# A two-block transformer kernel on one core: the mixer's value weights as ordinary tiles, and the last gate tiles and branch columns in another order

## The reference, cut to what matters

```
z = xn @ w_in[l]                       # 1024 -> 5952 columns
r, k, v, xw, xa, xg = ...              # shifted columns for the RWKV mixer
mq, mk, mv, mo, mi, mf = ...           # columns for the mLSTM mixer
y_a = _rwkv7_mixer(r, k, v, ...)       # a triangular system, solved in levels, then 4 chunks
y_b = _mlstm_mixer(mq, mk, mv, ...)    # 4 heads; mv are the values, needed as (token, column)
g_a, g_b = jnp.split(z_gate, 2, axis=-1)
u = jax.nn.sigmoid(g_a) * (y_a @ br_a[l]) + jax.nn.sigmoid(g_b) * (y_b @ br_b[l])
h = h + u @ w_out[l]
```

## Time and profile before

| what | us |
|---|---|
| time before, median of 3 runs | 2619.52 (2617.49 to 2622.0) |
| the profiled execution's own time | 2617.78 |
| its span in the trace | 2615.8 |
| mixer of layer 0, from tile 27's wait to L2133 | 1439.2 to 1471.5 of the span |
| the same in layer 1 | 2185.7 to 2216.4 |

### The profile page before, as it was taken

The page is one execution under the profiler, slowest core; times in us unless marked ns, Lnnn a source line. Parts: engine busy times, 40 slices in busy tenths (PEclk is TensorE's granted clock), DMA queues, the critical chain, the costliest instruction groups (busy, mean ns, idle before and its releaser), DMA issues.

```text
span 2615.8 us, 50326 instructions
## 1 busy us (share of the span) xinstructions
PE 2434.9 (93%) x20748; PEld 2207.6 (84%) x20748; DVE 1248.7 (48%) x1990; ACT 1002.4 (38%) x1594; POOL 224.7 (9%) x199
## 2 busy tenths in 40 slices
PE   7999799899989799999999799999999987989998
PEld 3754599799966599989998688899999977888998
DVE  1152355555424255465567353455555565443554
ACT  3153433354334353343345331334433454321433
POOL 0000000000000000010005231100100033321000
PEclk9999899989989999989999799999999998999999
DMA  6154354354424545345533112544445231114552
GB/s 256 70 176 174 144 190 172 128 183 178 160 81 166 189 169 191 146 164 186 184 112 108 55 67 106 212 181 180 164 174 191 105 129 65 66 67 161 201 184 96
DMA packets 64486, 388.05 MB, mean 148 GB/s; under 512 B 7152, under 2 KB 7280, under 8 KB 27376
## 3 DMA queue, kind: packets, MB, share of 16 engines
q1 hardware_dynamic: 63216, 379.61, 39.8%
q10 hardware_dynamic: 864, 5.16, 0.5%
q0 software_dynamic: 288, 1.57, 0.2%
HBM read 385.27 MB, written 1.05 MB: 148 GB/s over the span
## 4 chain that ended last, share of the span: by engine, by line
PE 79%; DVE 5%; issue 5%; POOL 4%; ACT 4%; DMA 2%; POOLq 0%; SPq 0%; DVEq 0%; ACTq 0%
PE ps L1707 19%; PE ps L1708 19%; PE ps L1709 19%; PE ps L1783 5%; POOL t_lo L555 3%; PE ps L1796 2%; PE ps L2221 2%; PE ps L2068 2%; DMA ring_a<-in_wa 2%; POOL h_lo L533 1%; PE ps L2259 1%; PE ps L1677 1%; PE ps L2194 1%; PE ps L1654 1%; PE ps L1811 1%
## 5 line engine op out<-in xcount | busy, mean ns | idle before, releaser
L1707 PE MATMUL ps<-h_hi,w_hi 128*128 128x256 f32 x2464 | 702.6, 285 | 12.4 <-DVE mod L1063 8.7
L1708 PE MATMUL ps<-h_lo,w_hi 128*128 128x256 f32 x2464 | 700.5, 284 | 0.0
L1709 PE MATMUL ps<-h_hi,w_lo 128*128 128x256 f32 x2464 | 700.5, 284 | 0.0
L1707 PEld LDWEIGHTS ps<-h_hi,w_hi 128*128 128x128 f32 x2464 | 476.6, 193 | 14.7 <-DVE mod L1063 9.6
L1708 PEld LDWEIGHTS ps<-h_lo,w_hi 128*128 128x128 f32 x2464 | 476.5, 193 | 0.1
L1709 PEld LDWEIGHTS ps<-h_hi,w_lo 128*128 128x128 f32 x2464 | 476.3, 193 | 0.0
L1125 DVE TENSOR_TENSOR w_lo<-ring_a,w_hi 128x1024 fp32r<-128x1024 f32 x308 | 366.4, 1231 | 30.0 <-ACT w_hi L634 29.8
L1708 PE MATMUL ps<-hid_lo,d_hi 128*128 128x256 f32 x1232 | 348.7, 283 | 0.0
L1707 PE MATMUL ps<-hid_hi,d_hi 128*128 128x256 f32 x1232 | 348.7, 283 | 0.0
L1709 PE MATMUL ps<-hid_hi,d_lo 128*128 128x256 f32 x1232 | 348.6, 283 | 0.0
L634 ACT CAST w_hi<-ring_a 128x1024 fp32r<-128x1024 f32 x308 | 306.0, 1044 | 61.9 <-DMA ring_a<-in_wa 61.9
(11 more groups left out here) (282 smaller groups left out, 3296.9 us busy)
## 6 DMA issues: line engine op xcount, KB each, us to landing
ring_a<-in_wa SPq DMA_DIRECT2D x278, 1024.0 KB, 4.8
ring_d<-in_wd SPq DMA_DIRECT2D x154, 512.0 KB, 5.3
work<-in_wa SPq DMA_DIRECT2D x6, 1024.0 KB, 21.7
work<-in_small POOLq DMA_DIRECT2D x2, 768.0 KB, 5.6
c<-in_c ACTq DMA_DIRECT2D x1, 1175.0 KB, 10.4
work<-in_c ACTq DMA_DIRECT2D x1, 1088.0 KB, 5.0
x<-in_x ACTq DMA_DIRECT2D x1, 1024.0 KB, 14.8
work<-in_ctx ACTq DMA_DIRECT2D x1, 1024.0 KB, 19.3
```

The lines of the kernel that those rows point to most:

```text
L1707: nc.tensor.matmul(out, hi, to_hi, start=start, stop=False, skip_group_check=True)
L1708: nc.tensor.matmul(out, hi, to_lo, start=False, stop=False, skip_group_check=True)
L1709: return nc.tensor.matmul(out, lo, to_hi, start=False, stop=stop, skip_group_check=True)
```

## The change

The value tiles 27 to 30 become ordinary tiles: TensorE's `tile` with the weights stationary, ScalarE's `empty_value` into the buffers `sg` and `hid` (`vraw`), then eight transposes into banks 6 and 7, and two copies by ScalarE into `mv` (`mvt`, `mv`). In layer 1 the places of the tiles are moved two ahead as well: tile 23 stands ahead of the head norms (`head_norms`), tiles 24 and 25 between the first transposes and the first `per_unit`. At the end of the mixer both last gate tiles stand ahead of y's transposes, and ScalarE empties both ahead of its root (`ysd`). The branch columns 0 to 3 of `y_b` follow the transposes in four banks. TensorE's wait for `hsd` ahead of the levels is gone.

```diff
-        ems = [v[:, i, :] for v in (sg, hid) for i in range(2)]
+        ems = vraw = [v[:, i, :] for v in (sg, hid) for i in range(2)]
...
-                def empty_values(t):
...
+                def empty_value(t):
+
+                    act.wait_ge(t_done, l * NT2 + t + 1)
+                    nc.scalar.copy(vraw[t - MV], ps[:, 4 + t % 2, 0:T]).then_inc(t_free, 1)
                     round_t(t + 2)
...
-                empty_t(23)
+                def empties(first, last):
+                    for t in range(first, last + 1):
+                        (empty_t if t < MV else empty_value)(t)
+
+                later = 2 * l
+                empties(23, 23 + later)
...
-                empty_values(MV)
+                empties(27 + later, 28)
...
-                empty_values(MV + 2)
+                empties(29, 29)
                 act.wait_ge(ml_v, MVS.at("c3", l))
                 nc.scalar.activation(nsq[:, :, :], nsq[:, :, :], ACT.Silu).then_inc(ml_a, 1)
+                empties(30, 30)
+                act.wait_ge(ml_p, MP.at("mvt", l))
+                for b in range(2):
+                    ins = nc.scalar.copy(mv[:, b, :], ps[:, 6 + b, :])
+                ins.then_inc(ml_a, 1)
...
                 empty_gate(gates_at("y", 0)[0])
+                empty_gate(gates_at("y", 1)[0])
                 act.wait_ge(rw_v, RV.at("s2", l))
...
-                empty_gate(gates_at("y", 1)[0])
...
-                    nc.vector.tensor_tensor(umix[:, n, :], ps[:, 4 + n % 2, 0:T], gate_a[:, n, :], ALU.mult)\
+                    nc.vector.tensor_tensor(umix[:, n, :], ps[:, 4 + n % 4, 0:T], gate_a[:, n, :], ALU.mult)\
...
+                if l:
+                    tile(23)
+                    head_norms()
                 pe.wait_ge(rw_a, RA.at("gg", l))
+                pe.wait_ge(rw_v, RV.at("rkr", l))
                 to_tokens(z[:, V0:V0 + QT, 1:T + 1], 6).then_inc(rw_p, 1)
-                tile(23)
+                if l == 0:
+                    tile(23)
+                else:
+                    tile(24)
+                    tile(25)
...
-                value_tiles(MV)
+                for t in range(n + 3, MV + 2):
+                    tile(t)
...
-                value_tiles(MV + 2)
-
+                tile(29)
+                tile(30)
+                pe.wait_ge(t_free, p0 + GATES)
+                pe.wait_ge(rw_v, RV.at("mt", l))
+                for b in range(2):
+                    for j in range(QT):
+                        mm = nc.tensor.transpose(ps[:, 6 + b, j * P:(j + 1) * P], vraw[j][:, b * P:(b + 1) * P], ident)
+                mm.then_inc(ml_p, 1)
...
-                pe.wait_ge(ml_a, MA.at("hsd", l))
...
                 tile(gates_at("y", 0)[0], bank=6)
-
-                pe.wait_ge(ml_v, MVS.at(f"yb{QT - 1}", l))
-                chunk_here(chunk0[f"br{l}"], chunk0[f"br{l}"] % 2)
-                pe.wait_ge(ch_v, CV.at("s", l * NC_ + NC_ - 1))
-                branch(0, 1)
-                branch(1, 1)
+                tile(gates_at("y", 1)[0], bank=6)
...
-                tile(gates_at("y", 1)[0], bank=6)
+                pe.wait_ge(ml_v, MVS.at(f"yb{QT - 1}", l))
+                pe.wait_ge(ch_v, CV.at("s", l * NC_ + NC_ - 1))
+                for n in range(4):
+                    if n == 2:
+                        pe.wait_ge(t_free, p0 + NT2)
+                    if n % 2 == 0:
+                        chunk_here(chunk0[f"br{l}"] + n // 2, (chunk0[f"br{l}"] + n // 2) % 2)
+                    branch(n, 1)
...
-                    if n >= 2:
+                    if n >= 4:
                         if n % 2 == 0:
                             chunk_here(c, c % 2)
-                        pe.wait_ge(br_free, l * KD + n - 1)
+                        pe.wait_ge(br_free, l * KD + n - 3)
                         branch(n, 1)
```

More of the change, by code:

```diff
@@ L349, in program @@
                     + [f"{n}{j}" for j in range(QT) for n in ("rec", "hs", "yb")])
-        MA = Steps(["ab", "ex", "ln", "silu", "hq", "hsd", "so"])
-        MP = Steps(["if", "mu", "var"])
+        MA = Steps(["ab", "ex", "ln", "silu", "mv", "hq", "hsd", "so"])
+        MP = Steps(["if", "mvt", "mu", "var"])
         n_id = {}
@@ L884, in empty_conv @@
                     round_t(t + 2)
-                def empty_values(t):
-                    act.wait_ge(t_done, l * NT2 + t + 2)
-                    both = ps[:, 5 if t == MV else 4, :].rearrange("p (b s n) -> p s b n", b=2, s=2)
-                    for u in range(2):
-                        j = t + u - MV
-                        nc.scalar.copy(mv[:, :, j * P:(j + 1) * P], both[:, (t + u) % 2]).then_inc(t_free, 1)
+                def empty_value(t):
+                    act.wait_ge(t_done, l * NT2 + t + 1)
+                    nc.scalar.copy(vraw[t - MV], ps[:, 4 + t % 2, 0:T]).then_inc(t_free, 1)
                     round_t(t + 2)
-                    round_t(t + 3)
                 def empty_gate(t):
@@ L1975, in tile @@
                     mm.then_inc(t_done, 1)
-                def value_tiles(t):
-                    pe.wait_ge(t_free, p0 + MV if t > MV else p0 + MV - 1)
-                    for u in range(2):
-                        for part in range(2):
-                            tile_here(t + u, part)
-                    for b in range(2):
-                        for k in range(KD):
-                            cols = slice(b * P, (b + 1) * P)
-                            out = ps[:, 5 if t == MV else 4, b * T:(b + 1) * T].rearrange("p (a n) -> p a n", n=P)
-                            for i, (act_, w) in enumerate(((h_hi, t_hi), (h_lo, t_hi), (h_hi, t_lo))):
-                                mm = nc.tensor.matmul(out, act_[:, k, cols], w[:, :, k, :],
-                                                      start=(k == 0 and i == 0), stop=(k == KD - 1 and i == 2))
-                    mm.then_inc(t_done, 2)
                 for t in range(4):
@@ L2034, in _, with head_norms @@
                     tile(t)
-                pe.wait_ge(rw_v, RV.at("rn", l))
-                if l:
-                    pe.wait_ge(vres_a, 1)
-                hr = const("headrow")
-                for j in range(QT):
-                    mm = nc.tensor.matmul(ps[:, j // 2, half(j)], hr[0:8, cols(j)], inv_norm, start=True, stop=True)
-                mm.then_inc(rw_p, 1)
-                pe.wait_ge(rw_v, RV.at("rkr", l))
-                for j in range(QT):
-                    mm = nc.tensor.matmul(ps[:, 2 + j // 2, half(j)], const("headones"), bon[:, j, :],
-                                          start=True, stop=True)
-                mm.then_inc(rw_p, 1)
+                def head_norms():
+                    pe.wait_ge(rw_v, RV.at("rn", l))
+                    if l:
+                        pe.wait_ge(vres_a, 1)
+                    hr = const("headrow")
+                    for j in range(QT):
+                        mm = nc.tensor.matmul(ps[:, j // 2, half(j)], hr[0:8, cols(j)], inv_norm, start=True, stop=True)
+                    mm.then_inc(rw_p, 1)
+                    pe.wait_ge(rw_v, RV.at("rkr", l))
+                    for j in range(QT):
+                        mm = nc.tensor.matmul(ps[:, 2 + j // 2, half(j)], const("headones"), bon[:, j, :],
+                                              start=True, stop=True)
+                    mm.then_inc(rw_p, 1)
+                if l == 0:
+                    head_norms()
                 tile(22)
@@ L2078, in _ @@
                 per_unit(2, kt, bh).then_inc(rw_p, 1)
-                tile(24)
+                n = 24 + 2 * l
+                tile(n)
                 pe.wait_ge(rw_v, RV.at("khc", l))
@@ L2084, in _ @@
                 per_unit(0, kh, rt).then_inc(rw_p, 1)
-                tile(25)
+                tile(n + 1)
                 pe.wait_ge(rw_v, RV.at("x1", l))
@@ L2089, in _ @@
                 per_unit(6, kh, kt).then_inc(rw_p, 1)
-                tile(26)
+                tile(n + 2)
                 pe.wait_ge(rw_v, RV.at("mrt", l))
                 to_tokens(bhc, 0).then_inc(rw_p, 1)
-                value_tiles(MV)
+                for t in range(n + 3, MV + 2):
+                    tile(t)
                 pe.wait_ge(rw_v, RV.at("art", l))
@@ L2220, in branch @@
                     for k in range(QT):
-                        mm = nc.tensor.matmul(ps[:, 4 + n % 2, part * T:(part + 1) * T],
+                        mm = nc.tensor.matmul(ps[:, 4 + n % 4, part * T:(part + 1) * T],
                                               ring_a[:, c % 2, n % 2, part * QT + k, :], y[:, k, :],
```

13 lines of the change are left out of this document (9 added, 4 removed).

## The result

The changed kernel takes 2594.17 us in the median of four runs (2586.96 to 2597.84), the kernel before 2619.42 in the same comparison (2617.49 to 2622.0). The ratio is 0.990 with a 95% interval of 0.9877 to 0.9923: the change makes the kernel faster, by 25.3 us. The forecast was 2581 with a range of 2570 to 2593. The direction was right, the gain a third smaller than said, and the time 1.2 us above the range.

A forecast was written before the change was run, and what follows sets the result against it. TensorE, busy 93%, was taken to lose time only in waits and at its lower clock, chiefly in the two-tile value chain. Five terms summed to -37.3 us from 2617.78, giving 2580.5, stated as 2581, range 2570 to 2593.

The forecast's parts named there:

- Term 1: Layer 0's value stage: single tiles end TensorE's waits for GpSimd and shrink the one for the silu; -16.3 us.
- Term 2: Layer 1's value stage: tiles 22 and 23 fill the head norms' wait, VectorE becomes the bound; -17.3 us.
- The taps on VectorE end at 1448.3 as before; nothing ahead of them moves.: Step for layer 0's value stage: VectorE's taps keep their old end time; part of the -16.3 us.
- I take it that the first `per_unit` starts when it did: Step for layer 1: the first per-unit products keep their start, with two tiles less to come; part of -17.3 us.
- Term 3: Levels in both layers: removing TensorE's wait for ScalarE's root `hsd` saves 4.2 us, at least 2.
- Term 4: Y stage: late root, slow transposes and a chunk wait, against a filled `y_a` wait; +1.0 us per layer, +2.0 together.
- The rule of the Trainium skill that I weighed: Y stage, ScalarE's table switch: 1.28 us load plus 1.38 drain, making the sum 2.8 us worse; rival at 2583, chance 0.05.
- Term 5: Layer 0's heads: a shorter wait ahead may keep TensorE's clock high; -1.5 us, between 0 and -6.5.
- signs of being wrong: Value stages: taps or ln later than said, layer 1's first `per_unit` slipping, or the clock falling where it was high; unpriced.
- A new wait in the y stage and in the layer 1 chain: Rival: root, chunk and low clock cost 6 us in each layer instead of 1; 2591 us, chance 0.12.

The follow-up runs named there:

- e1: Changed kernel with GpSimd doing only a quarter of the rests of value tiles 29 to 31, so work is left out; 2584.8 us.
- e7: Changed kernel with ScalarE emptying tile 30 ahead of the silu, which moves tile 32's rounding and rest up too; 2596.1 us.
- e6: Changed kernel with TensorE's wait for `hsd` ahead of the levels put back in both layers; 2596.1 us.
- b3: Changed kernel with gates' chain before tap 3, tile 30's emptying and value copies before the silu, TensorE's silu wait later, y's root before the last sigmoid; 2576.15 us.
- e4: Changed kernel with layer 1's value tiles in the places that layer 0 has, without the shift; 2598.2 us.

## Why the prediction was right or wrong

The time lies above the range because terms 1 and 2 gave 24.6 us where 33.6 were forecast. The step that failed in both is that VectorE's side was carried over from the trace of before with its times, as if nothing ran beside it. By the marks, against the profiled execution before (in brackets the forecast):

- **Term 1, layer 0's value stage: -12.4 (-16.3).** The single tiles did what was said: TensorE ran tiles 27 to 30 from 1440.7 to 1453.6 without a wait for GpSimd. The step that failed is "The taps on VectorE end at 1448.3 as before; nothing ahead of them moves." They started 1.75 us later, since tile 18 ran at the low clock in this trace, and took 6.1 us longer. The silu ended 4.4 us late by that account, the transposes ran at the low clock (1.96 instead of 1.04), L2144 waited for the gates' last instruction, itself 1.1 longer. e1 gives these microseconds back, e7 adds to them. The term was mis-sized by 3.9; its mechanism, single tiles in place of two stalls, held.
- **Term 2, layer 1: -12.2 (-17.3),** taken from tile 18 on. Two causes: "I take it that the first `per_unit` starts when it did" was 2.7 us off in this trace, because tiles 24 and 25 need rests just when VectorE multiplies with two SBUF inputs; and the taps took 13.97 us instead of 11.90. The gates' chain behind them took 4.6 us where 4.3 was said. Together these are the 5.1 us that the term lacks.
- **Term 3, the wait for `hsd`: -4.4 (-4.2).** Right: e6's marks give it back with 2.2 us in each layer.
- **Term 4, the y stage: +2.8 (+2.0).** Right in each step, though over all traces the sum is nearer to +1.6: wait 3.64 (3.6), transposes at half clock, if shorter, 3.06 (3.8), chunk 1.48 (1.4), none for `y_a`. The rule of the Trainium skill that I weighed (ScalarE: Activation LUTs, "What ACT_TABLE_LOAD costs") is not borne out: the root followed its load at once (1.28 us, then the root 0.01 us behind), with no drain of 1.38.
- **Term 5, the clock in the heads: 0 (-1.5).** In layer 0 it is 16.2 us from L2144 to the end of tile 31, before 16.1: the low clock stayed there, as the earlier trace rows had it, behind a wait of 4.88 us and not of the 2.3 forecast. e1, with a wait of 2.02, had 14.2. So one trace has the gain that the term weighed; whether the shorter wait alone brings it is not shown.
- What no term had: +1.75 in layer 0 ahead of the tokens, where tile 18 ran at the low clock, +0.9 between the mixers, +0.9 in the first head (nearly all in layer 1), -1.4 in layer 1's first levels, where the kernel before had a granted clock of 0.76 behind its wait (2263 to 2270 us) and the same pieces in layer 0 had 1.00, and -0.1 behind the last mixer. The sum -12.4 - 12.2 - 4.4 + 2.8 + 1.75 + 0.9 + 0.9 - 1.4 - 0.1 is -24.2, the difference of the spans.

Of the miss of 13, 9 us lie in the taps and the rests of tiles 24 and 25, one mechanism that no rival named. The prediction did list both places as signs of being wrong ("if the taps or ln came later than said, if the first `per_unit` in layer 1 slipped"), without a price or a cause. The trace of before already held the price: the slow tap of 1580 ns above was there to be read, and tile 28's rest took 2.66 us beside the taps. The rival "A new wait in the y stage and in the layer 1 chain" came near the time (2591), but mostly by luck: it put 12 us on the root, the chunk and a low clock in the y stage, which took 2.8 by the marks. Only the delay of layer 1's chain, which it names, did come.

## What to carry to other kernels

When a change lets one engine run ahead, ask what it will now run beside, and read min and max of the instructions there, not the mean: one slow instance in the trace of before is the price, and the number of meetings is what the change multiplies. A chain's duration may be carried over from a trace only with its neighbours. Where GpSimd subtracts beside VectorE's two-input work, either put the work on VectorE itself (1.28 us against 2.04 here), or order VectorE's program so that what the next engine needs stands ahead of the work that suffers.

## What was unexpected of the hardware

- A GpSimd subtraction of 128x512 beside taps costs VectorE 1.02 us each time, and VectorE's short one-input instruction suffers too: the 4x256 `TENSOR_SCALAR` took 1.39 us where it started together with a rest, and 0.28 in e1, where none ran beside it.
- The turn is not always fair. In b3's third tap eight taps ran at full pace and the GpSimd instruction beside them lasted 4457 ns. The views of the taps and of GpSimd (ns min/median/max):

```profile
L1463 DVE SCALAR_TENSOR_TENSOR nsq<-work,vec,nsq x8: 462/464/465, 1454.7 to 1457.4; 128x253 f32<-128x253 f32 x8
...
L555 POOL TENSOR_TENSOR t_lo<-ring_a,t_hi x2: 1443/2950/4457, 1453.2 to 1454.6; 128x512 fp32r<-128x512 f32 x2
```

In the changed kernel three of the third tap's eight instructions did wait for GpSimd. What decides it stays open; it was not tried.
- The runs of the changed kernel scatter by 11 us, and those of the kernel before by 4.5 to 14, according to the group of runs. Much of it goes with the clock's dips in the attention block: from 125 to 300 us the granted clock was 0.93 in the changed kernel and 0.91 in e4, from 300 to 450 us 0.96 and 0.93, and e4 left the block 6.5 us later. What makes the dips differ stays open.
